# Ten instead of nine seven-product quads in each pair of column blocks, with a third sum buffer and one raw buffer fewer

## The chip, the core and the metric

The kernel runs on one core of a Trainium2 chip. The metric is the device time of one execution in microseconds (us), the median of several runs. The engines are PE (TensorE, matmuls), DVE (VectorE), ACT (ScalarE), POOL (GpSimd) and SP (SyncE, which here only issues DMAs).

## What is computed

One encoder layer for 256 positions of width 4096. The reference in its parts that matter here:

```python
h = layer_norm(x, emb_ln_g, emb_ln_b)                  # (256, 4096)
proj = h @ w_in[l]                                     # (4096, 22080 columns)
q_a, kv_a, dq, dk, dv, g_mla, g_dswa, r_mla, r_dswa = jnp.split(proj, IN_OFFSETS, axis=-1)
a = mla_attention(q_a, kv_a, ...)
y_mla = (a * silu(g_mla)) @ w_o_mla[l]
b = dilated_mixture(dq, dk, dv, rel_bias)
y_dswa = (b * silu(g_dswa)) @ w_o_dswa[l]
out = (sigmoid(r_mla) * y_mla + sigmoid(r_dswa) * y_dswa) @ w_out[l]
h = layer_norm(DEEPNORM_ALPHA * h + out, ln_g[l], ln_b[l])
```

The change is all in the big product `h @ w_in`, for 34 of its blocks of 512 columns.

## The kernel before

**Precision.** Every fp32 product is made of three matmuls on operands split into a high part and a rest: high times high, high times low, low times high. For a weight tile ACT writes the high part (`q_hi`), DVE then subtracts it from the raw tile and writes the rest (`q_low`, in the same bytes as `q_raw`).

**Pairs and quads.** 34 column blocks are taken as 17 pairs (p = 0 to 16). The 4096 rows of the weights are taken in 16 steps for each pair (q = 0 to 15), so that a step, a *quad*, is a 2x2 arrangement of products: two halves of the positions by two column blocks, over two row tiles of 128. The number of a quad over all pairs is g = 16p + q; its raw weights are one load of 1 MB into `q_raw[g % RAWS]`. A quad is done in one of two ways:

- *direct* (`direct_quad`): eight products, 24 matmuls of 128x512;
- *seven-product* (`seven_quad`, Strassen-Winograd): seven products, 21 matmuls. It wants three sums of the quad's weights (the first made in place by an accumulating DMA that POOL issues, `first_sum`; the others by two DVE subtractions, `quad_sums`, into `q_sum`), their high part on ACT and their rest on DVE (`q_sum_low`), and sums of the left operand (`t_hi`, `t_lo`), made once ahead of the pairs by `t_values`, one piece for each q in `SEVEN`.

`SEVEN` lists the q that are done with seven products: nine of the sixteen. Results gather in two sets of four PSUM banks. After a pair ACT copies the first of them out, and DVE combines the rest in `mixed_out` and `direct_out`, four adds each.

**What sets the order.** Each engine's program is written out in order; semaphores join them. SP issues the load of quad g when the raw buffer is free: `raw_free`, after the matmuls of quad g - RAWS that read `q_low` (for q = 0 after all of that quad). POOL issues the accumulating DMA of a seven-product quad when its load has landed. DVE takes for each g: the sums of quad g+1 if that is a seven-product quad (`sums_late` puts them behind instead for one q), then in q = 2 `direct_out` of the pair before, then `quad_low(g)`. `quad_low` waits for ACT's `quad_high(g)`, which waits until PE has done quad g-3 (three `q_hi` buffers). PE waits for `q_lo_ready` at the start of each quad.

**The first pair** starts while the section before it ("start") ends, so its raw buffers come free one by one: buffers that share bytes with that section's weight ring wait for `slot_done`, the one that holds the latent keys waits for `kva_stored`, the last, over `qa_sb`, for `qa_stored`. **After the last pair** the section "gates" begins; ACT may write the fourth slot of its ring only when the last pair's `c_fourth` is stored (`fourth_stored`), and POOL reads latent keys and queries back.

## Time and profile before

| | us |
|---|---|
| median of 3 runs | 2677.81 (2677.27 to 2680.55) |
| the profiled execution | 2677.33 |
| its span, first to last instruction | 2675.5 |
| PE busy | 2640.5 (99%) |
| DVE busy | 2061.1 (77%) |
| ACT busy | 1352.8 (51%) |
| granted TensorE clock, mean over the span | 0.996 |

The profiled execution takes 1.8 us more than its span. Matmuls are pipelined: one of 128x512 is shown with 389 ns, but the next starts 227 ns after it, so PE's pace is read from starts, or from a stretch divided by its matmuls. The pairs run from 175.71 us to 1559.08 us of the span.

### The profile page before, as it was taken

Reading aid. Unit: us, or ns where it says so; the run is one execution under the profiler, and the core shown is the slowest. Engines: PE = TensorE matmul, PEld = TensorE weight load, DVE = VectorE, ACT = ScalarE, POOL = GpSimd, SP = SyncE. Lnnn points to the kernel's source line nnn. Section 1 sums busy time; section 2 is a strip of 40 time slices with the busy share of each in tenths; the row PEclk is TensorE's granted clock in tenths of the full one; section 3 lists DMA queues with packets and bytes.
Section 4 is the critical chain, followed back from the end, with each engine's and each line's share of the span. In section 5 each row is a group of like instructions: output and inputs, shape, how many; then the busy total and the mean of one; then the engine's idle time right before and its main releaser. Section 6 shows DMA issues by size and latency. Waiting matters only on the chain.

```text
span 2675.5 us, 32812 instructions
## 1 busy us (share of the span) xinstructions
PE 2640.5 (99%) x12300; PEld 2205.5 (82%) x12300; DVE 2061.1 (77%) x1970; ACT 1352.8 (51%) x1295; POOL 264.4 (10%) x371
## 2 busy tenths in 40 slices
PE   7999999999999999999999999999999999999998
PEld 5878888888888888888888889988888888888886
DVE  7769888898888898888898876765565566656557
ACT  5445555555555555555555555544444444433333
POOL 0010111101111101111101101110100100110000
PEclk9999999999999999999999999999999999999998
DMA  6587887878888888888788864356776777777765
GB/s 206 168 288 222 256 261 246 248 237 256 256 252 252 240 244 258 253 253 253 235 243 263 249 213 126 128 173 207 236 244 181 232 224 232 249 235 220 229 216 177
DMA packets 240264, 612.89 MB, mean 229 GB/s; under 512 B 17513, under 2 KB 34261, under 8 KB 240004
## 3 DMA queue, kind: packets, MB, share of 16 engines
...
## 4 chain that ended last, share of the span: by engine, by line
PE 95%; DVE 2%; DMA 1%; issue 1%; ACT 0%; SPq 0%; DVEq 0%; ACTq 0%
PE acc L608 13%; PE acc L610 13%; PE acc L609 13%; PE bank L632 4%; PE bank L628 4%; PE bank L633 4%; PE acc L633 3%; PE acc L628 3%; PE acc L632 3%; PE acc L667 3%; PE acc L671 3%; PE bank L667 3%; PE acc L670 3%; PE bank L670 3%; PE bank L671 3%; PE acc L616 3%
## 5 line engine op out<-in xcount | busy, mean ns | idle before, releaser
L1020 ACT ACTIVATE q_hi<-q_raw 128x2048 fp32r<-128x2048 f32 x272 | 522.3, 1921 | 545.5 <-PE bank L617 155.7
L1223 DVE TENSOR_TENSOR w_lo<-w_raw,w_hi 128x1024 fp32r<-128x1024 f32 (+2 forms) x448 | 504.5, 1139 | 295.1 <-ACT w_hi L979 292.1
L1306 DVE TENSOR_TENSOR q_low<-q_raw,q_hi 128x2048 fp32r<-128x2048 f32 x272 | 621.2, 2284 | 5.2 <-ACT q_hi L1020 5.2
L979 ACT ACTIVATE w_hi<-w_raw 128x1024 fp32r<-128x1024 f32 (+2 forms) x448 | 430.9, 982 | 299.2 <-PE acc L610 253.4
L608 PE MATMUL acc<-w_hi,oper_hi 128*128 128x512 f32 (+1 forms) x1072 | 410.7, 383 | 3.2 <-DVE w_lo L1223 3.1
L610 PE MATMUL acc<-w_hi,oper_lo 128*128 128x512 f32 (+1 forms) x1072 | 405.6, 378 | 0.0
L609 PE MATMUL acc<-w_lo,oper_hi 128*128 128x512 f32 (+1 forms) x1072 | 405.2, 378 | 0.0
L1310 DVE TENSOR_TENSOR q_sum_low<-q_sum,q_hi 128x1536 fp32r<-128x1536 f32 x153 | 267.6, 1749 | 0.0
L1824 POOL DMA_DIRECT2D q_raw<-q_raw x153 | 131.1, 857 | 1207.2 <-DMA q_raw<-in_w_in 1207.2
L1023 ACT ACTIVATE q_hi<-q_sum 128x1536 fp32r<-128x1536 f32 x153 | 227.4, 1487 | 16.2 <-DVE q_sum L1298 0.5
L608 PEld LDWEIGHTS acc<-w_hi,oper_hi 128*128 128x128 f32 x1072 | 201.3, 188 | 41.6 <-DVE w_lo L1223 5.2
L610 PEld LDWEIGHTS acc<-w_hi,oper_lo 128*128 128x128 f32 x1072 | 201.2, 188 | 37.6
L609 PEld LDWEIGHTS acc<-w_lo,oper_hi 128*128 128x128 f32 x1072 | 201.4, 188 | 35.8
L1295 DVE TENSOR_TENSOR q_sum<-q_raw 128x512 f32<-128x512 f32 x153 | 105.6, 690 | 121.2 <-PE bank L617 58.6
L1298 DVE TENSOR_TENSOR q_sum<-q_raw,q_sum 128x1024 f32<-128x1024 f32 x153 | 187.5, 1225 | 5.2
L632 PE MATMUL bank<-q_hi,oper_hi 128*128 128x512 f32 x432 | 168.0, 389 | 0.0
L633 PE MATMUL bank<-q_hi,oper_lo 128*128 128x512 f32 x432 | 168.0, 389 | 0.0
L632 PE MATMUL acc<-q_hi,oper_hi 128*128 128x512 f32 x384 | 149.4, 389 | 0.0
L633 PE MATMUL acc<-q_hi,oper_lo 128*128 128x512 f32 x384 | 149.4, 389 | 0.0
L628 PE MATMUL bank<-q_low,oper_hi 128*128 128x512 f32 x432 | 106.7, 389 | 0.0
L608 PE MATMUL acc<-w_hi,am_hi 128*128 128x512 f32 x256 | 103.2, 403 | 0.0
L610 PE MATMUL acc<-w_hi,am_lo 128*128 128x512 f32 x256 | 100.0, 391 | 0.0
...
## 6 DMA issues: line engine op xcount, KB each, us to landing
q_raw<-in_w_in SPq DMA_DIRECT2D x256, 1024.0 KB, 6.1
w_raw<-in_w_in SPq DMA_DIRECT2D x128, 512.0 KB, 4.5
w_raw<-in_w_out SPq DMA_DIRECT2D x128, 512.0 KB, 3.9
q_raw<-q_raw POOLq DMA_DIRECT2D x153, 256.0 KB, 5.3
...
```

Of the source, the lines that this page charges most:

```text
L608: pe.matmul(y, hi[:, k, tok(t)], wh, start=first, stop=False)
L609: pe.matmul(y, hi[:, k, tok(t)], wl, start=False, stop=False)
L610: ins = pe.matmul(y, lo[:, k, tok(t)], wh, start=False, stop=last)
L628: ins = pe.matmul(banks[2 * i + t], oper_hi[:, 2 * q + a, tok(t)], raw_lo[:, 2 * a + i, :], start=False, stop=False)
L632: pe.matmul(y, oper_hi[:, k, tok(t)], hi[:, 2 * a + i, :], start=False, stop=False)
L633: ins = pe.matmul(y, oper_lo[:, k, tok(t)], hi[:, 2 * a + i, :], start=False, stop=q == QUADS - 1 and a == 1)
L979: act.activation(w_hi[:, n % RING, 0:w], w_raw[:, n % RING, 0:w], ACT.Copy).then_inc(w_hi_ready, 1)
L1020: act.activation(q_hi[h][:, 0:4, :], q_raw[r][:, :, :], ACT.Copy).then_inc(q_hi_ready, 1)
L1023: act.activation(q_hi[h][:, 4:7, :], q_sum[sevens_before(g) % 2][:, :, :], ACT.Copy).then_inc(q_hi_ready, 1)
L1223: dve.tensor_tensor(w_lo[:, n % RING, 0:w], w_raw[:, n % RING, 0:w], w_hi[:, n % RING, 0:w].bitcast(F32), ALU.subtract).then_inc(w_lo_read ...
L1306: dve.tensor_tensor(q_low[r], q_raw[r], q_hi[h][:, 0:4, :].bitcast(F32), ALU.subtract).then_inc(q_lo_ready, 1)
L1310: dve.tensor_tensor(q_sum_low[m], q_sum[m], q_hi[h][:, 4:7, :].bitcast(F32), ALU.subtract).then_inc(q_lo_ready, 1)
```

## The change

`SEVEN` gets ten entries, (2, 3, 4, 6, 7, 8, 10, 11, 12, 14) for (2, 4, 5, 7, 8, 10, 11, 13, 14). In the first pair three of them (2, 3, 4) stay direct, so it has seven such quads and not nine. Over all pairs there are 167 and not 153. The sums get a third buffer, which takes the bytes of one raw buffer; raw buffers go from six to five. What lay over the bytes of the raw buffer that is gone (the latent keys) is read back later, after quad 270. The store of a pair's results is issued in q = 7 and not 8 of the next pair, since it goes by `SEVEN[4]`.

```diff
-SEVEN = (2, 4, 5, 7, 8, 10, 11, 13, 14)
+SEVEN = (2, 3, 4, 6, 7, 8, 10, 11, 12, 14)
 NQ = PAIRS * QUADS
-RAWS, HIS = 6, 3
-KVA_RAW, QA_RAW = 2, RAWS - 1
+RAWS, HIS, SUMS = 5, 3, 3
+QA_RAW = RAWS - 1
+FIRST_DIRECT = (2, 3, 4)
+
+
+def sevens(p):
+
+    return tuple(q for q in SEVEN if p or q not in FIRST_DIRECT)
 
 
 def is_seven(g):
 
-    return g % QUADS in SEVEN
+    return g % QUADS in sevens(g // QUADS)
...
-T_STEPS = (("qa0", 5), ("qa0", 8), ("qa0", 11), ("qa0", 14), ("kva0", 3), ("kva0", 6), ("kva0", 9), ("kva0", 12), ("kva1", 12))
+T_STEPS = (("qa0", 5), ("qa0", 8), ("qa0", 11), ("qa0", 14), ("kva0", 3), ("kva0", 6), ("kva0", 9), ("kva0", 12), ("kva1", 10), ("kva1", 13))
...
-        q_raw = [sb(f"q_raw{n}", at_, [P, 4, CW]) for n, at_ in enumerate((R_B, R_B + 8 * K, R_C + 16 * K, RINGS + 32 * K, RINGS + 40 * K, R_C + 24 * K))]
+        q_raw = [sb(f"q_raw{n}", at_, [P, 4, CW]) for n, at_ in enumerate((R_B, R_B + 8 * K, RINGS + 32 * K, RINGS + 40 * K, R_C + 24 * K))]
...
-        q_sum = [sb(f"q_sum{n}", SMALL + 3328 + n * 6 * K, [P, 3, CW]) for n in range(2)]
+        q_sum = [sb(f"q_sum{n}", at_, [P, 3, CW]) for n, at_ in enumerate((SMALL + 3328, SMALL + 3328 + 6 * K, R_C + 16 * K))]
...
                     if g == 0:
                         sp.wait_ge(rows_stored, 16)
-                    elif g == KVA_RAW:
-                        sp.wait_ge(kva_stored, 32)
-                    elif g in (3, 4):
-                        sp.wait_ge(slot_done, SEC["start"].per_slot - (2 if g == 3 else 0))
+                    elif g in (2, 3):
+                        sp.wait_ge(slot_done, SEC["start"].per_slot - (2 if g == 2 else 0))
                     elif g == QA_RAW:
                         sp.wait_ge(qa_stored, 32)
...
-                if m >= 2:
-                    before = [n for n in range(g) if is_seven(n)][-2]
+                if m == SUMS - 1:
+                    dve.wait_ge(kva_stored, 32)
+                if m >= SUMS:
+                    before = [n for n in range(g) if is_seven(n)][-SUMS]
                     dve.wait_ge(quad_done, before + 1)
...
-                    sums_late = q == SEVEN[0] + 1 if p else q == 1
+                    sums_late = q == SEVEN[0] + 1 and p > 0
...
-                if g == SEVEN[0]:
+                if g == 0:
                     pool.wait_ge(acc_free, 4)
                     pool.dma_start(qa_d[:, :, CW:2 * CW], qa_sb[:, :, CW:2 * CW]).then_inc(qa_stored, 16)
                 if g >= QUADS and g % QUADS == SEVEN[4]:
                     store_pair(g // QUADS - 1)
-            for buffer in (KVA_RAW, QA_RAW):
-                last_user = NQ - 1 - (NQ - 1 - buffer) % RAWS
-                pool.wait_ge(raw_free, last_user - last_user // QUADS)
-                if buffer == QA_RAW:
-                    pool.dma_start(qa_sb[:, :, :], qa_d[:, :, :]).then_inc(qa_loaded, 16)
-                else:
-                    pool.dma_start(kva_hi[:, :, :].bitcast(F32), kva_d[:, 0, :, :]).then_inc(kva_loaded, 16)
-                    pool.dma_start(kva_lo[:, :, :].bitcast(F32), kva_d[:, 1, :, :]).then_inc(kva_loaded, 16)
+            last_user = NQ - 1 - (NQ - 1 - QA_RAW) % RAWS
+            pool.wait_ge(raw_free, last_user - last_user // QUADS)
+            pool.dma_start(qa_sb[:, :, :], qa_d[:, :, :]).then_inc(qa_loaded, 16)
+            pool.wait_ge(quad_done, NQ - 1)
+            pool.dma_start(kva_hi[:, :, :].bitcast(F32), kva_d[:, 0, :, :]).then_inc(kva_loaded, 16)
+            pool.dma_start(kva_lo[:, :, :].bitcast(F32), kva_d[:, 1, :, :]).then_inc(kva_loaded, 16)
             store_pair(PAIRS - 1)
```

How this moves instructions shows best at three places. The first is DVE's program in the first pair, from the second quad's `q_low1` on; the number behind a name is the buffer's. Before:

```order
L1306 TENSOR_TENSOR q_low1_72<-q_raw1_66,q_hi2_79 128x2048
L1347 COPY qa_sb_97<-acc1 128x2x512
L1295 TENSOR_TENSOR q_sum0_80<-q_raw2_67 128x512
L1298 TENSOR_TENSOR q_sum0_80<-q_raw2_67,q_sum0_80 128x1024
L1306 TENSOR_TENSOR q_low2_73<-q_raw2_67,q_hi1_78 128x2048
L1310 TENSOR_TENSOR q_sum_low0_82<-q_sum0_80,q_hi1_78 128x1536
L1295 TENSOR_TENSOR q_sum1_81<-q_raw4_69 128x512
L1298 TENSOR_TENSOR q_sum1_81<-q_raw4_69,q_sum1_81 128x1024
L1306 TENSOR_TENSOR q_low3_74<-q_raw3_68,q_hi2_79 128x2048
L1295 TENSOR_TENSOR q_sum0_80<-q_raw5_70 128x512
L1298 TENSOR_TENSOR q_sum0_80<-q_raw5_70,q_sum0_80 128x1024
L1306 TENSOR_TENSOR q_low4_75<-q_raw4_69,q_hi0_77 128x2048
```

and of the changed kernel:

```order
L1312 TENSOR_TENSOR q_low1_71<-q_raw1_66,q_hi2_77 128x2048
L1353 COPY qa_sb_97<-acc1 128x2x512
L1312 TENSOR_TENSOR q_low2_72<-q_raw2_67,q_hi1_76 128x2048
L1312 TENSOR_TENSOR q_low3_73<-q_raw3_68,q_hi2_77 128x2048
L1312 TENSOR_TENSOR q_low4_74<-q_raw4_69,q_hi0_75 128x2048
L1301 TENSOR_TENSOR q_sum0_78<-q_raw1_66 128x512
L1304 TENSOR_TENSOR q_sum0_78<-q_raw1_66,q_sum0_78 128x1024
L1312 TENSOR_TENSOR q_low0_70<-q_raw0_65,q_hi1_76 128x2048
L1301 TENSOR_TENSOR q_sum1_79<-q_raw2_67 128x512
L1304 TENSOR_TENSOR q_sum1_79<-q_raw2_67,q_sum1_79 128x1024
```

The sums of quads 2, 4 and 5 are gone; the first sums are those of quad 6 (`q_sum0<-q_raw1`), and they stand ahead of quad 5's `q_low0`.

The second is DVE's program around the end of a pair, here from pair 0 to pair 1. `c_first`, `c_third` and `c_fourth` are the targets of `mixed_out` (from `acc` here) and `direct_out` (from `bank`). Before:

```order
L1317 TENSOR_TENSOR c_first_84<-c_first_84,acc0 128x512
L1319 TENSOR_TENSOR c_third_85<-c_first_84,acc1 128x512
L1321 TENSOR_TENSOR c_first_84<-c_first_84,acc1 128x512
L1322 TENSOR_TENSOR c_fourth_86<-c_third_85,acc1 128x512
L1295 TENSOR_TENSOR q_sum1_81<-q_raw0_65 128x512
L1298 TENSOR_TENSOR q_sum1_81<-q_raw0_65,q_sum1_81 128x1024
L1306 TENSOR_TENSOR q_low5_76<-q_raw5_70,q_hi1_78 128x2048
L1330 TENSOR_TENSOR c_fourth_86<-bank3,c_fourth_86 128x512
L1331 TENSOR_TENSOR c_third_85<-bank2,c_third_85 128x512
L1332 TENSOR_TENSOR c_first_84<-bank0,c_first_84 128x512
L1333 TENSOR_TENSOR c_first_84<-bank1,c_first_84 128x512
L1306 TENSOR_TENSOR q_low0_71<-q_raw0_65,q_hi2_79 128x2048
```

and of the changed kernel:

```order
L1301 TENSOR_TENSOR q_sum1_79<-q_raw3_68 128x512
L1304 TENSOR_TENSOR q_sum1_79<-q_raw3_68,q_sum1_79 128x1024
L1312 TENSOR_TENSOR q_low2_72<-q_raw2_67,q_hi1_76 128x2048
L1301 TENSOR_TENSOR q_sum2_80<-q_raw4_69 128x512
L1304 TENSOR_TENSOR q_sum2_80<-q_raw4_69,q_sum2_80 128x1024
L1336 TENSOR_TENSOR c_fourth_86<-bank3,c_fourth_86 128x512
L1337 TENSOR_TENSOR c_third_85<-bank2,c_third_85 128x512
L1338 TENSOR_TENSOR c_first_84<-bank0,c_first_84 128x512
L1339 TENSOR_TENSOR c_first_84<-bank1,c_first_84 128x512
L1312 TENSOR_TENSOR q_low3_73<-q_raw3_68,q_hi2_77 128x2048
L1316 TENSOR_TENSOR q_sum_low1_82<-q_sum1_79,q_hi2_77 128x1536
```

Quad 3 of a pair is now a seven-product quad, and its sums (`q_sum2<-q_raw4`) stand between `q_low2` of quad 1 and `direct_out`.

The third is SP's queue of loads at the first pair. Before:

```order
L564 DMA q_raw0_65<-in_w_in 128x2x1024 [waits rows_stored]
L564 DMA q_raw1_66<-in_w_in 128x2x1024
L564 DMA q_raw2_67<-in_w_in 128x2x1024 [waits kva_stored]
L564 DMA q_raw3_68<-in_w_in 128x2x1024 [waits slot_done]
L564 DMA q_raw4_69<-in_w_in 128x2x1024 [waits slot_done]
L564 DMA q_raw5_70<-in_w_in 128x2x1024 [waits qa_stored]
L564 DMA q_raw0_65<-in_w_in 128x2x1024 [waits quad_done]
L564 DMA q_raw1_66<-in_w_in 128x2x1024 [waits raw_free]
```

and of the changed kernel:

```order
L568 DMA q_raw0_65<-in_w_in 128x2x1024 [waits rows_stored]
L568 DMA q_raw1_66<-in_w_in 128x2x1024
L568 DMA q_raw2_67<-in_w_in 128x2x1024 [waits slot_done]
L568 DMA q_raw3_68<-in_w_in 128x2x1024 [waits slot_done]
L568 DMA q_raw4_69<-in_w_in 128x2x1024 [waits qa_stored]
L568 DMA q_raw0_65<-in_w_in 128x2x1024 [waits quad_done]
L568 DMA q_raw1_66<-in_w_in 128x2x1024 [waits raw_free]
```

Buffer 2 no longer waits for `kva_stored`; the buffer over `qa_sb` is now the fifth, not the sixth, and the first buffer to be used again is that of quad 5, not quad 6.

## Rows read from the trace of the kernel before

**Rows 1.** The page: the chain that ended last, by engine.

```profile
PE 95%; DVE 2%; DMA 1%; issue 1%; ACT 0%; SPq 0%; DVEq 0%; ACTq 0%
```

**Rows 2.** Busy by stretch, first two pairs: PE, PEld, DVE, ACT, POOL; clock, DMA, GB/s.

```profile
175.71:264.20 88.49, 83.39 (x358) 68.53 (x357) 72.95 (x51) 44.26 (x26) 9.28 (x11) 0.96 0.81 245
264.20:345.12 80.92, 80.92 (x358) 67.03 (x357) 72.46 (x52) 44.41 (x26) 9.38 (x12) 1.00 0.82 250
```

**Rows 3.** Chain of work in the first pair, 189 to 203 us: start, us, what.

```profile
183.70 5.67 DMA q_raw<-in_w_in
...
189.66 8.15 DMA q_raw<-q_raw
...
197.84 0.70 DVE q_sum L1295
...
199.71 2.29 DVE q_low L1306
...
202.05 1.22 PE acc L667 x2
```

**Rows 4.** Timeline of PE in the first pair: its one long idle stretch.

```profile
202.05 0.79 PE L667 MATMUL acc<-q_low,oper_hi 128*128 128x512 f32 x1 [5.09 <-DVE q_low L1306]
```

**Rows 5.** Busy time by stretch, as rows 2: the stretch at half clock.

```profile
199.90:206.60 6.70, 4.55 (x11) 3.59 (x12) 6.70 (x4) 3.21 (x2) 0.01 (x1) 0.50 0.75 180
```

**Rows 6.** Timeline of DVE from quad 1 to quad 3 of pair 6.

```profile
664.19 0.69 DVE L1317 TENSOR_TENSOR c_first<-c_first,bank 128x512 f32<-128x512 f32 x1 [1.14 <-ACT c_first L1031]
...
666.84 0.68 DVE L1295 TENSOR_TENSOR q_sum<-q_raw 128x512 f32<-128x512 f32 x1
...
668.70 2.29 DVE L1306 TENSOR_TENSOR q_low<-q_raw,q_hi 128x2048 fp32r<-128x2048 f32 x1
670.90 0.69 DVE L1330 TENSOR_TENSOR c_fourth<-acc,c_fourth 128x512 f32<-128x512 f32 x1
...
673.30 2.28 DVE L1306 TENSOR_TENSOR q_low<-q_raw,q_hi 128x2048 fp32r<-128x2048 f32 x1
675.50 1.75 DVE L1310 TENSOR_TENSOR q_sum_low<-q_sum,q_hi 128x1536 fp32r<-128x1536 f32 x1
677.16 2.28 DVE L1306 TENSOR_TENSOR q_low<-q_raw,q_hi 128x2048 fp32r<-128x2048 f32 x1
```

**Rows 7.** Timeline of PE: first matmuls of quads 14 and 15 of pair 5.

```profile
658.60 0.39 PE L667 MATMUL bank<-q_low,oper_hi 128*128 128x512 f32 x1
...
663.36 0.39 PE L628 MATMUL acc<-q_low,oper_hi 128*128 128x512 f32 x1
```

**Rows 8.** Timeline of SP: the loads that these two quads set free, and one earlier.

```profile
654.94 0.37 SPq L564 DMA_DIRECT2D q_raw<-in_w_in  x1
...
659.70 0.37 SPq L564 DMA_DIRECT2D q_raw<-in_w_in  x1
...
665.37 0.37 SPq L564 DMA_DIRECT2D q_raw<-in_w_in  x1
```

**Rows 9.** Timeline of POOL: the accumulating DMA of pair 6's quad 2.

```profile
655.48 0.85 POOL L1824 DMA_DIRECT2D q_raw<-q_raw  x1 [19.50 <-DMA q_raw<-in_w_in]
```

**Rows 10.** DMA issues of 654 to 656.5 us: KB, us from issue to landing.

```profile
q_raw<-in_w_in SPq DMA_DIRECT2D x1, 1024.0 KB, 5.6
q_raw<-q_raw POOLq DMA_DIRECT2D x1, 256.0 KB, 6.3
```

**Rows 11.** Issue to landing, all loads (L564) and all accumulating DMAs (L1824).

```profile
DMA to landing us min/median/max: 3.7/5.9/11.1
...
DMA to landing us min/median/max: 3.2/5.3/9.9
```

**Rows 12.** DVE's waits: who waited for whom, us in total, times, longest.

```profile
DVE q_sum L1295 <- DMA q_raw<-q_raw: 8.6, 3, 6.8
```

**Rows 13.** Timelines at the first "gates" slots: POOL's store, the matmul that waits.

```profile
1561.04 0.55 POOL L1834 DMA_DIRECT2D pair_blocks<-c_fourth  x1 [15.11 <-ACT c_fourth L1038]
...
1567.45 0.50 PE L608 MATMUL acc<-w_hi,oper_hi 128*128 128x512 f32 x1 [0.21 <-DVE w_lo L1223]
```

More of the change, by code:

```diff
@@ L316, in program @@
         R_A = RINGS + 48 * K
-        R_B = R_A + 40 * K
+        R_B = R_A + 44 * K
         R_C = R_B + 16 * K
@@ L339, in program @@
         t_val = sb("t_val", R_A + (4 * len(SEVEN) + 2) * K, [P, 4, P])
-        q_raw = [sb(f"q_raw{n}", at_, [P, 4, CW]) for n, at_ in enumerate((R_B, R_B + 8 * K, R_C + 16 * K, RINGS + 32 * K, RINGS + 40 * K, R_C + 24 * K))]
-        q_low = [sb(f"q_low{n}", at_, [P, 4, CW], F32R) for n, at_ in enumerate((R_B, R_B + 8 * K, R_C + 16 * K, RINGS + 32 * K, RINGS + 40 * K, R_C + 24 * K))]
+        q_raw = [sb(f"q_raw{n}", at_, [P, 4, CW]) for n, at_ in enumerate((R_B, R_B + 8 * K, RINGS + 32 * K, RINGS + 40 * K, R_C + 24 * K))]
+        q_low = [sb(f"q_low{n}", at_, [P, 4, CW], F32R) for n, at_ in enumerate((R_B, R_B + 8 * K, RINGS + 32 * K, RINGS + 40 * K, R_C + 24 * K))]
         q_hi = [sb(f"q_hi{n}", at_, [P, 7, CW], F32R) for n, at_ in enumerate((R_C, RINGS, RINGS + 14 * K))]
-        q_sum = [sb(f"q_sum{n}", SMALL + 3328 + n * 6 * K, [P, 3, CW]) for n in range(2)]
-        q_sum_low = [sb(f"q_sum_low{n}", SMALL + 3328 + n * 6 * K, [P, 3, CW], F32R) for n in range(2)]
+        q_sum = [sb(f"q_sum{n}", at_, [P, 3, CW]) for n, at_ in enumerate((SMALL + 3328, SMALL + 3328 + 6 * K, R_C + 16 * K))]
+        q_sum_low = [sb(f"q_sum_low{n}", at_, [P, 3, CW], F32R) for n, at_ in enumerate((SMALL + 3328, SMALL + 3328 + 6 * K, R_C + 16 * K))]
         c_first = sb("c_first", R_A + 4 * len(SEVEN) * K, [P, 2, CW])
@@ L652, in seven_quad @@
                 raw_lo, hi = q_low[g % RAWS], q_hi[hi_buffer(g)]
-                sum_lo = q_sum_low[sevens_before(g) % 2]
-                first, last = n == 0, n == len(SEVEN) - 1
+                sum_lo = q_sum_low[sevens_before(g) % SUMS]
+                first, last = q == sevens(p)[0], n == len(SEVEN) - 1
                 p2, p3, p4, x = direct_banks(p)
@@ L682, in column_pairs @@
                     for q in range(QUADS):
-                        if q in SEVEN:
+                        if is_seven(p * QUADS + q):
                             seven_quad(p, q)
@@ L1022, in quad_high @@
                     act.wait_ge(sums_ready, sevens_before(g) + 1)
-                    act.activation(q_hi[h][:, 4:7, :], q_sum[sevens_before(g) % 2][:, :, :], ACT.Copy).then_inc(q_hi_ready, 1)
+                    act.activation(q_hi[h][:, 4:7, :], q_sum[sevens_before(g) % SUMS][:, :, :], ACT.Copy).then_inc(q_hi_ready, 1)
             def first_product_out(p):
@@ L1289, in quad_sums @@
                 r, m = g % RAWS, sevens_before(g)
-                raw, out_ = q_raw[r], q_sum[m % 2]
+                raw, out_ = q_raw[r], q_sum[m % SUMS]
                 dve.wait_ge(s1_made[r], first_sums(g))
-                if m >= 2:
-                    before = [n for n in range(g) if is_seven(n)][-2]
+                if m == SUMS - 1:
+                    dve.wait_ge(kva_stored, 32)
+                if m >= SUMS:
+                    before = [n for n in range(g) if is_seven(n)][-SUMS]
                     dve.wait_ge(quad_done, before + 1)
@@ L1307, in quad_low @@
                 if is_seven(g):
-                    m = sevens_before(g) % 2
+                    m = sevens_before(g) % SUMS
                     dve.wait_ge(q_hi_ready, splits_before(g) + 2)
```

## The prediction

> **What bounds the kernel now.** I read the page first: PE has 95% of the chain that ended last [rows 1]. So what counts is how many matmuls PE does, and whether anything makes it wait that did not before. Then the busy time by stretch, cut at the pairs [rows 2]: the second pair takes 80.92 us, all of it busy, and it has 9 x 21 + 7 x 24 = 357 matmuls, so one costs 226.7 ns (the view counts one more that laps over the edge). I take all later pairs to be like it. A seven-product quad is thus 4.76 us, a direct one 5.44 us. The first pair takes 88.49 us for the same work: 7.57 us are lost there. The chain in that pair [rows 3] shows where: the load of quad 5 issued at 183.70, its accumulating DMA from 189.66 for 8.15 us, the sums, then `q_low` of quad 4, and PE starts quad 4 at 202.05 after 5.09 us of idleness [rows 4]. Right behind, the granted clock is half, that is 1.2 GHz, for 6.7 us [rows 5]. Since 7.57 is more than the idle time, the clock has the rest.
>
> **The change, part by part.**
>
> *Matmuls.* In 16 pairs one more quad is seven-product: 16 x 3 x 0.2267 = **-10.88 us**. In the first pair two fewer are: 2 x 3 x 0.2267 = **+1.36 us**. A later pair then has 354 matmuls, 80.24 us; the first 363, 82.28 us.
>
> *DVE's load.* From DVE's timeline [rows 6], start to start: sums 1.86 us (666.84 to 668.70), `q_low` 2.20, `q_sum_low` 1.66 (675.50 to 677.16), `mixed_out` 2.65 (664.19 to 666.84), `direct_out` 2.40. A pair has 16 `q_low`, and 10 times the sums and their rest: 35.2 + 35.2 + 5.1 = 75.5 us against PE's 80.24. That fits, with 4.8 us to spare (before 72.0 of 80.92). In a run of three seven-product quads DVE needs 3 x 5.72 = 17.2 us to PE's 14.3, but with the direct quad behind it 19.4 to 19.7, so a run is made good. Going through a pair by these durations, with ACT's high part following PE's end of quad g-3, `q_low` ends 0.9 to 3 us ahead of PE's need (0.9 in quad 5, about 1.2 in quads 7 and 9) if the sums' data are there. The third buffer lets the third sum of a run start before the first is used up. I cost DVE's own work at nothing; its cover is these 0.9 us.
>
> *The raw buffers.* This is where it can go wrong. A load is issued 1.10 us after the start of the seven-product quad that frees its buffer (658.60, 659.70), 2.01 us after that of a direct one (663.36, 665.37) [rows 7, 8]. Now it is freed by quad g-5, not g-6, so each load starts some 5 us later against its use. Let T be the time from that issue to the landing of the accumulating DMA. Then sums take 1.9 us (from 189.66 + 8.15 = 197.81, to 199.71), and PE starts 2.34 us after `q_low` starts (202.05) [rows 3]: 4.2 us together, and they concern PE's quad g-1, since the sums of g stand ahead of `q_low(g-1)`. So for quads 6, 10 and 14 (buffer freed by a direct quad, four quads until the need, one of them direct): T may be 4.76 x 3 + 5.44 - 2.01 - 4.2 = 13.5 us. For quads 7, 8, 11 and 12: 14.4 us. For quad 3 `direct_out` comes in between too: 4.76 + 3 x 5.44 - 1.10 - 4.2 - 2.4 = 13.4 us. Quads 2 and 4 have more.
>
> What T is: a load takes 5.9 us in the median, an accumulating DMA 5.3, and 0.3 us lie between (183.70 + 5.67 to 189.66) [rows 3, 11]: 11.5 us. The slower ones show why: the accumulating DMA of quad 2 lands at 655.48 + 6.3, the load issued beside it at 654.94 + 5.6 [rows 8 to 10], so it comes 1.3 us behind the next load. T is then the distance of two loads (4.5 to 5.7 us), a load, and 1.3 us. With a load of 5.9 that is 11.7 to 12.9 us, under every limit; with one of 7 it is 12.8 to 14.0 and passes that of quad 3 (distance 5.7) by 0.6; with the longest accumulating DMA, 9.9, T is 16.1. Before, DVE waited for such a DMA three times in all, 6.8 of 8.6 us in the wait above [rows 12], so nothing of this showed. The DMA engines were busy for 0.82 of a pair [rows 2] and get a tenth accumulating DMA. Bounds for a later pair: 0 (T stays at 12.9), and 2.6 us (16.1 against 13.5; a stall gives the loads behind it time, so within a pair the largest excess counts, not the sum). The rows lie nearer to the lower end. I take 0.4 us a pair, a quarter of the pairs late by 1 to 2 us: 16 x 0.4 = **+6.4 us**.
>
> A page speaks on the same point. The Trainium skill (DMA: Bandwidth & Descriptors, section Anatomy of one DMA) gives a DMA about 2.0 us and its bytes at 436 GB/s. By that, called an estimate, a load is 4.4 us, the accumulating one 2.6, T 7.3, and no pair would ever wait: the sum would be 6.4 us lower. The trace does not agree: 5.9 and 5.3 in the median. The same page of the Trainium skill (section Latency and other measured facts) has HBM latency rise from 0.2 to 2 us under high load, which speaks against a change that adds traffic and removes a buffer; the longest load here, 11.1 us, fits that.
>
> *The first pair.* The 7.57 us go, since the sums of quads 2, 4 and 5 do: **-7.57 us**. What is late next is quad 6. Its sums stand ahead of quad 5's `q_low`. The load of quad 4 still waits for the stored queries, until 183.7, as quad 5's did [rows 3]; quads 5 and 6 follow within 1 us; that of quad 7 comes at 188.6 (quad 2 starts at 175.71 + 2 x 5.44, plus 2.01). Quad 6 is the third of three loads, so I put its landing near 194.4, its accumulating DMA 1.3 us behind the load of quad 7, at 199.5. PE would need quad 5 at 175.71 + 5 x 5.44 = 202.9, and gets it at 199.5 + 4.2 = 203.7. I take **+1.0 us**. Bounds: 0 (landing before 198.7), and with 8.15 us [rows 3] for the DMA from 194.7 it is 202.9 + 4.2 - 202.9 = 4.2, to which 2.5 (7.57 - 5.09) come if the clock falls again.
>
> *The tenth `t_values`* adds some 2.5 us of DVE work ahead of the pairs, which lies beside the last slots of "start"; `q_low` of quad 0 should end near 174.9, under 1 us ahead of PE. Cost 0; without that cover up to 1 us.
>
> *The end.* POOL reads the latent keys back at about 1553 us and not earlier, 1 MB on the queue in which `c_fourth` is stored at 1561.04; the fourth slot already waits for that store, 0.21 us [rows 13]. At 5.9 us, a 1 MB load's median [rows 11], the keys have landed by then. I take **+0.3 us** (0 to 2.6).
>
> Sum: -10.88 + 1.36 - 7.57 + 1.0 + 6.4 + 0.3 = **-9.4 us**. From the profiled execution's 2677.33 that is 2667.9. The median of the runs shown is 0.5 us higher, so I predict **2668.4 us** (-0.35%).
>
> **The rivals.**
>
> *All hidden.* The accumulating DMAs come in time in every pair, and at the first pair too. For it: a T of 11.5 by the medians. Against it: quad 3 needs its neighbour's load under 6.4 us. Sum: -10.88 + 1.36 - 7.57 + 0.3 = -16.8, 2661.0 us.
>
> *The first pair stalls as before.* Its accumulating DMA takes its 8.15 us and the clock falls: 4.2 + 2.5 instead of 1.0, 2674.1 us. For it: three loads bunch up behind the stored queries exactly as before. Against it: two accumulating DMAs fewer run beside them. The Trainium skill (TensorE: Matmul & The Clock Gate, section Terms) reckons a throttled stretch at its length times the share of pulses lost, here 6.7 x 0.5 = 3.4 us; rows 2 and 4 give 2.5, since PE was idle for part of it. By the page this case would end 0.9 us later.
>
> *The gain is eaten.* T exceeds its limit by about a microsecond in most pairs, 1.0 us each: 9.6 us more than in the forecast, 2678 us, no change. For it: quads 10 to 12 come in a run behind the 1 MB of stores that POOL issues in quad 7, with only quad 9 direct to let the queues empty.
>
> *Slower.* The same mechanism where every pair is late by 1.6 us at one quad: 16 x 1.6 = 25.6 for 6.4, 2687.6 us. It decides from 1.3 us a pair on (+5.4 us over before); T would have to be 14.8 us in each pair, where the medians add up to 11.5.
>
> *DVE becomes the bound.* By the sum above it cannot unless its operations grow by 6%; I give it no chance of its own.
>
> **How the numbers follow.** A measurement of this kernel tells some 0.2%, 5.4 us, from no change. Forecast (small waits, -5.4 to -14) 0.48; all hidden 0.20; first pair as before 0.06; gain eaten 0.18; slower 0.08. Faster is the first two and a third of the next: 0.70. Same 0.22. Slower 0.08. For 8 in 10 the range goes from the all-hidden case, 2660.5, to where half of "gain eaten" is in, 2677.0. The forecast's own range is 2663.5 to 2672.
>
> **What would show it.** In the changed profile: matmuls in the pairs fewer by 42; a later pair of 80.24 us where nothing waits, and PE idle ahead of a `q_low` matmul at quads 2, 5, 9 or 10 where it does, with DVE's sums waiting for `q_raw<-q_raw`; the first pair near 83.3 us with at most a short idle stretch at quad 5 and the clock at 1.00; the pairs' end some 10 us earlier. The prediction is wrong if later pairs stand above 81 us, if the clock falls again in the first pair, or if "gates" waits for its fourth slot by more than 1 us.

## The result and the profile after

The changed kernel takes 2691.60 us in the median of seven runs (2685.40 to 2700.58), the kernel before 2677.97 us in eight runs. An eighth run of the changed kernel, disturbed (6877.29 us), is left out; with it the median would be 2693.89. The ratio is 1.0053, with an interval of 1.0040 to 1.0066. It is slower by half a per cent, where I had predicted 2668.4 us. The profiled execution is one of the slower ones, 2696.74 us with a span of 2694.9.

The page of the changed kernel, the chain that ended last:

```profile
PE 73%; DMA 12%; DVE 11%; issue 3%; ACT 0%; SPq 0%; DVEq 0%; ACTq 0%
```

Against [rows 1] PE has lost 22 points of the chain, to DMA and DVE. Busy time by stretch, columns as [rows 2]: the first pair, the second, and the other fifteen.

```profile
175.65:259.13 83.48, 83.16 (x365) 67.84 (x363) 65.36 (x45) 40.99 (x24) 8.40 (x10) 1.00 0.83 252
259.13:341.20 82.07, 81.00 (x355) 66.21 (x354) 75.61 (x55) 45.38 (x27) 10.23 (x13) 1.00 0.85 250
341.20:1577.97 1236.77, 1216.59 (x5312) 994.32 (x5311) 1133.33 (x809) 695.21 (x427) 153.16 (x196) 1.00 0.83 247
```

The first pair takes 83.48 us, near the forecast's 83.3, with the clock at full speed. The later sixteen take 82.07 + 1236.77 = 1318.84 us where their matmuls need 16 x 80.24 = 1283.8. So 35.0 us are lost there, 2.2 us a pair, and I had put down 0.4. It is not a quarter of the pairs that are late: 15 of the 16 lose something, from 0.7 to 6.7 us. The waits of the changed kernel (who waited for whom, us in total, times, longest) say for what:

```profile
ACT q_hi L1027 <- DVE q_sum L1304: 94.7, 57, 7.1
ACT q_hi L1024 <- DMA q_raw<-q_raw: 86.4, 29, 5.8
DVE q_sum L1301 <- DMA q_raw<-q_raw: 55.7, 39, 5.5
...
PE acc L671 <- DVE q_low L1312: 6.6, 7, 1.8
PE bank L632 <- DVE q_low L1312: 6.1, 9, 2.3
PE acc L632 <- DVE q_low L1312: 4.8, 8, 0.9
PE bank L671 <- DVE q_low L1312: 3.8, 6, 1.8
```

DVE waits 39 times for an accumulating DMA, 55.7 us, where [rows 12] has 3 times and 8.6 us. The three before are all in the first pair; of the 39 now, 36 are in later pairs. Behind DVE, PE stands still for 21.3 us. Issue to landing, all loads and then all accumulating DMAs of the changed kernel, beside [rows 11]:

```profile
DMA to landing us min/median/max: 3.6/5.8/11.7
...
DMA to landing us min/median/max: 3.2/6.3/10.8
```

An accumulating DMA takes 1.0 us more in the median than before (6.3 for 5.3), a load 0.1 less. I paired each load with its accumulating DMA in both traces. T, from the load's issue to the accumulated landing, has in the later pairs a median of 11.8 us before (144 quads, 22 of them over 13.4 us, longest 16.5) and 12.0 us after (160 quads, 45 over 13.4, longest 17.3). So the whole time has hardly grown, and long ones were there before. This is the longest of the kernel before, quad 11 of pair 14: SP's timeline, POOL's timeline, the DMA issues at 1350.3, and DVE's timeline.

```profile
1343.10 0.37 SPq L564 DMA_DIRECT2D q_raw<-in_w_in  x1
...
1350.29 0.86 POOL L1824 DMA_DIRECT2D q_raw<-q_raw  x1 [1.86 <-DMA q_raw<-in_w_in]
...
q_raw<-q_raw POOLq DMA_DIRECT2D x1, 256.0 KB, 9.4
...
1361.99 0.69 DVE L1295 TENSOR_TENSOR q_sum<-q_raw 128x512 f32<-128x512 f32 x1 [0.61 <-PE bank L617]
```

The data landed at 1350.29 + 9.4 = 1359.7 us, 16.6 us after 1343.10, and DVE came for them 2.3 us later. The sixth raw buffer had covered 16.5 us without a trace in any table of waits.

What a late DMA does now is seen in the changed kernel's pair 13, which begins at 1252.77 us. DVE's timeline, and then the matmul at which PE waits, the first of quad 5:

```profile
1256.30 0.69 DVE L1301 TENSOR_TENSOR q_sum<-q_raw 128x512 f32<-128x512 f32 x1 [1.35 <-DMA q_raw<-q_raw]
...
1258.17 0.68 DVE L1336 TENSOR_TENSOR c_fourth<-bank,c_fourth 128x512 f32<-128x512 f32 x1
...
1260.57 2.28 DVE L1312 TENSOR_TENSOR q_low<-q_raw,q_hi 128x2048 fp32r<-128x2048 f32 x1
...
1264.43 2.28 DVE L1312 TENSOR_TENSOR q_low<-q_raw,q_hi 128x2048 fp32r<-128x2048 f32 x1
...
1270.35 2.29 DVE L1312 TENSOR_TENSOR q_low<-q_raw,q_hi 128x2048 fp32r<-128x2048 f32 x1
...
1276.09 2.28 DVE L1312 TENSOR_TENSOR q_low<-q_raw,q_hi 128x2048 fp32r<-128x2048 f32 x1
...
1278.43 1.89 PE L632 MATMUL acc<-q_low,oper_hi 128*128 128x512 f32 x7 [0.34 <-DVE q_low L1312]
```

The sums of quad 3 start when their data land. From there DVE has no idle time worth the name until `q_low` of quad 5 at 1276.09, 19.8 us later, and PE follows 2.34 us behind. PE could have begun quad 5 at 1252.77 + 2 x 5.44 + 3 x 4.76 = 1277.93. So the data of quad 3 had to land by 1277.93 - 2.34 - 19.8 = 1255.8. Its load was issued at about 1243.7 (1.10 us after the start of quad 14): T may be 12.1 us here and not 13.4. In this pair T was 12.6, and quad 5 begins 0.5 us late.

The same holds in all sixteen later pairs. What T of quad 3 has above 12.1 us is, to some 0.1 us, what PE loses at the starts of quads 2, 4 and 5 together:

| pair | T of quad 3 | above 12.1 | lost at quads 2, 4 and 5 |
|---|---|---|---|
| 15 | 10.5 | 0 | 0.0 |
| 8 | 12.0 | 0 | 0.0 |
| 13 | 12.6 | 0.5 | 0.5 |
| 10 | 13.0 | 0.9 | 0.9 |
| 6 | 14.4 | 2.3 | 2.2 |
| 5 | 15.2 | 3.1 | 3.0 |

Up to 13.3 us all of it is lost at quad 5; what is above that is lost at quad 2. This is 14.6 us of the 35.0. Another 7.4 us go in quads 6 and 7 (a loss in a quad is what its start and that of the next are too far apart), for the data of quad 8: its accumulating DMA is the next that POOL issues behind the stores of the pair before, its T has a median of 14.8 us against my limit of 14.4, and PE is late in the six pairs where it is over 15.5.

The clock fell once in the later pairs, behind the longest of these waits. PE's timeline, and a stretch behind it:

```profile
720.40 2.51 PE L632 MATMUL bank<-q_low,oper_hi 128*128 128x512 f32 x8 [2.33 <-DVE q_low L1312]
...
722.00:725.00 3.00, 3.00 (x9) 2.32 (x8) 3.00 (x2) 2.46 (x2) 0.00 (x0) 0.50 0.39 72
```

Granted 0.50, 1.2 GHz. The two quads there, the one before the wait's end and the one behind it, took 7.25 and 7.18 us for 4.76 and 5.44: 4.2 us over, of which 2.33 are idle time.

At the first slots of "gates", the answer to [rows 13], POOL's timeline, two of its DMA issues with KB and us to landing, and PE's timeline:

```profile
1572.83 0.54 POOL L1859 DMA_DIRECT2D kva_hi<-latent_keys  x1 [7.83 <-PE bank L621]
1573.36 0.53 POOL L1860 DMA_DIRECT2D kva_lo<-latent_keys  x1
1579.76 0.55 POOL L1840 DMA_DIRECT2D pair_blocks<-c_fourth  x1 [5.87 <-ACT c_fourth L1042]
...
kva_lo<-latent_keys POOLq DMA_DIRECT2D x1, 512.0 KB, 9.5
...
pair_blocks<-c_fourth POOLq DMA_DIRECT2D x1, 256.0 KB, 5.3
...
1587.44 0.50 PE L612 MATMUL acc<-w_hi,oper_hi 128*128 128x512 f32 x1 [1.31 <-DVE w_lo L1227]
```

The wait is 1.31 us, 1.1 more than before.

### The profile page after: what moved, and what is told of

Same layout as the page of the kernel before. It is cut to its first block, busy times and chain, and to the rows that moved or that the text cites. A ratio compares the mean times of both kernels' runs of the same rounds, so it can differ in the third digit from the quotient of the medians.

```text
span 2694.9 us, 32834 instructions
## 1 busy us (share of the span) xinstructions
PE 2643.2 (98%) x12258; PEld 2192.8 (81%) x12258; DVE 2107.4 (78%) x2018; ACT 1366.3 (51%) x1310; POOL 276.6 (10%) x385
## 3 DMA queue, kind: packets, MB, share of 16 engines
q0 software_dynamic: 41936, 105.84, 16.5%
## 4 chain that ended last, share of the span: by engine, by line
PE 73%; DMA 12%; DVE 11%; issue 3%; ACT 0%; SPq 0%; DVEq 0%; ACTq 0%
PE acc L612 13%; PE acc L614 13%; PE acc L613 13%; DMA q_raw<-q_raw 7%; DMA q_raw<-in_w_in 5%; DVE q_low L1312 4%; PE bank L632 2%; PE bank L637 2%; PE bank L636 2%; DVE q_sum_low L1316 2%; PE acc L671 2%; PE bank L671 2%; PE acc L632 2%; PE acc L636 2%; PE acc L637 2%
## 5 line engine op out<-in xcount | busy, mean ns | idle before, releaser
L1027 ACT ACTIVATE q_hi<-q_sum 128x1536 fp32r<-128x1536 f32 x167 | 247.8, 1484 | 95.3 <-DVE q_sum L1304 94.7
L1316 DVE TENSOR_TENSOR q_sum_low<-q_sum,q_hi 128x1536 fp32r<-128x1536 f32 x167 | 292.4, 1751 | 0.0
L1830 POOL DMA_DIRECT2D q_raw<-q_raw x167 | 143.1, 857 | 1201.8 <-DMA q_raw<-in_w_in 1201.8
L1304 DVE TENSOR_TENSOR q_sum<-q_raw,q_sum 128x1024 f32<-128x1024 f32 x167 | 204.6, 1225 | 5.8
L1301 DVE TENSOR_TENSOR q_sum<-q_raw 128x512 f32<-128x512 f32 x167 | 114.7, 687 | 56.5 <-DMA q_raw<-q_raw 55.7
L636 PE MATMUL bank<-q_hi,oper_hi 128*128 128x512 f32 x384 | 150.1, 391 | 0.0
L637 PE MATMUL bank<-q_hi,oper_lo 128*128 128x512 f32 x384 | 150.1, 391 | 0.0
L636 PE MATMUL acc<-q_hi,oper_hi 128*128 128x512 f32 x320 | 124.5, 389 | 0.0
L637 PE MATMUL acc<-q_hi,oper_lo 128*128 128x512 f32 x320 | 124.5, 389 | 0.0
L632 PE MATMUL bank<-q_low,oper_hi 128*128 128x512 f32 x384 | 97.0, 395 | 6.1 <-DVE q_low L1312 6.1
```

The source lines that it names most:

```text
L632: ins = pe.matmul(banks[2 * i + t], oper_hi[:, 2 * q + a, tok(t)], raw_lo[:, 2 * a + i, :], start=False, stop=False)
L636: pe.matmul(y, oper_hi[:, k, tok(t)], hi[:, 2 * a + i, :], start=False, stop=False)
L637: ins = pe.matmul(y, oper_lo[:, k, tok(t)], hi[:, 2 * a + i, :], start=False, stop=q == QUADS - 1 and a == 1)
L1027: act.activation(q_hi[h][:, 4:7, :], q_sum[sevens_before(g) % SUMS][:, :, :], ACT.Copy).then_inc(q_hi_ready, 1)
L1316: dve.tensor_tensor(q_sum_low[m], q_sum[m], q_hi[h][:, 4:7, :].bitcast(F32), ALU.subtract).then_inc(q_lo_ready, 1)
```

## The experiments

Twelve kernels, each timed beside the kernel before, which took 2676.4 to 2677.8 us in the medians. The changed kernel's 2691.60 us, with which they are compared below, was timed beside 2677.97. The expectations of the first four call the theory A: accumulated data come late, by more than DVE's slack can make good. I had not yet settled whether buffers, order or queue make them late.

**e1, DVE adds the direct products ahead of the sums.**

```
+ if p and q == 2: direct_out(p - 1)
  if g + 1 < NQ and is_seven(g + 1) and not sums_late: quad_sums(g + 1)
- if p and q == 2: direct_out(p - 1)
```

> One edit to the changed kernel: in q = 2 of a pair DVE does direct_out of the pair before ahead of the sums of quad 3, not behind them. Theory A (late data passed on): DVE has no idle time from the landing of quad 3's accumulating DMA to quad 5's q_low, so what it waits there reaches PE at quad 5; direct_out needs nothing of that DMA and fills the wait of about 1.4 us. The losses at quads 1, 4 and 5 of the later pairs (3.8 + 10.4 + 2.4 us in the profile of the changed kernel) go for the most part: 10 to 16 us faster than the changed kernel, about 2680 us. Rival B (DVE simply has too much work in a pair): the work is the same, no change, 2690 to 2697 us. Rival C (the stores in quad 7 are the cause): no change, quads 6 to 10 lose as before.

2681.64 us (2674.94 to 2689.18), ratio 1.001 (1.000 to 1.002): 10 us of the 14 come back. With DVE doing its 2.4 us of additions while it waits for quad 3's data, it is less behind at quad 5. The profile is of the slowest of its eleven runs (2689.18): even there the loss in quad 1 is gone (3.8 us in the changed kernel), and quads 4 and 5 together lose 10.1 us for 12.8. What is left stands in quads 4 to 7 and in 12 and 13.

**e2, the stores of a pair's results one seven-product quad later in POOL's queue.**

```
- if g >= QUADS and g % QUADS == SEVEN[4]:
+ if g >= QUADS and g % QUADS == SEVEN[5]:
```

> One edit to the changed kernel: POOL issues the store of the pair before behind the accumulating DMA of quad 8 instead of quad 7. Rival C (the stores stand ahead of quad 8's accumulating DMA in POOL's queue, 14.8 us from load issue to its landing in the median): that time falls by 2 to 3 us and the losses at quads 8 to 10 (7.6 us in all) go, 5 to 8 us faster, about 2687 us. Theory A gives the same sign with less, since quad 4 and 5 (12.8 us) stay: 0 to 5 us faster. Rival B: no change.

2709.39 us (2697.94 to 2711.61), ratio 1.0121 (1.0106 to 1.0137), 18 us slower than the changed kernel. The profile is of the fastest of its four runs (2697.94), so it shows little of that. In it the losses in quads 6 and 7 are gone (7.4 us over all pairs in the changed kernel, 0 here), with T of quad 8 down from 14.8 to 13.7 us in the median, but 3.2 us more are lost in quad 4, 3.6 more in quad 12, and 1 to 1.5 more in quads 1 and 9. Moving the stores moves the late quads. Why the sum grows I have not settled.

**e3, six raw buffers and two sum buffers, with the changed kernel's ten quads.** The sums of the third quad of a run then wait until the first is used up, and stand behind `q_low`.

```
- RAWS, HIS, SUMS = 5, 3, 3
+ RAWS, HIS, SUMS = 6, 3, 2
- sums_late = q == SEVEN[0] + 1 and p > 0
+ sums_late = q + 1 in (4, 8, 12)
```

> The changed kernel with six raw buffers and two sum buffers again; the sums of the third quad in a run (4, 8, 12) are made behind q_low of the second, since their buffer is free only then. Ten seven-product quads a pair stay. Theory A (five raw buffers make the data late): loads are issued a quad earlier, PE has nothing to wait for, later pairs take 80.24 us, 2661 to 2666 us, 10 us and more below the kernel before. Rival B (DVE has too much work): later pairs stay above 81.5 us, 2685 us and more, the more so with fewer sum buffers.

2712.14 us (2711.95 to 2712.26), ratio 1.0128 (1.0113 to 1.0144). My number fell, but for another reason than late data. The waits:

```profile
DVE q_sum L1302 <- PE bank L624: 33.7, 26, 1.7
DVE q_sum L1302 <- PE acc L624: 30.9, 24, 1.7
...
PE bank L635 <- DVE q_low L1313: 17.6, 26, 0.7
PE acc L635 <- DVE q_low L1313: 16.2, 24, 0.7
```

DVE waits 50 times for PE, and PE 50 times for DVE: three runs of three in each pair, the same 0.7 us each time, and every later pair takes 83.3 to 83.5 us. T was up to 19.6 us in this kernel, and no sum waited for it in any pair but the first. So a run of three, with its third sums behind `q_low`, does need the third sum buffer, which is what the change had bought with the raw one.

**e4, no accumulating DMAs.** It leaves out the first of the three weight sums of each seven-product quad; DVE, and ACT likewise, wait for the load alone.

```
- if is_seven(g):
-     first_sum(g)
...
- dve.wait_ge(s1_made[r], first_sums(g))
+ dve.wait_ge(q_loaded[r], quad_arrivals(g))
```

> The changed kernel without the accumulating DMAs: the first weight sum of each seven-product quad is left out (its output is not that of the reference), DVE and ACT wait for the load alone. DVE, ACT and PE do the same work. Theory A: the data come 5 to 7 us earlier, no waits in later pairs, 80.24 us each, about 2661 us. Rival B: DVE's work is what it was, pairs at 81.5 us and more, 2690 us. If it lies between, both have a part.

2660.68 us (2660.05 to 2661.05), ratio 0.9936 (0.9923 to 0.9950). The sixteen later pairs by stretch:

```profile
257.88:1541.88 1284.00, 1284.00 (x5666) 1063.22 (x5665) 1204.78 (x863) 733.95 (x454) 27.28 (x51) 1.00 0.64 222
```

1284.00 us, all of it busy. DVE is busy for 94% of it (1204.78) and holds nobody up. So the changed kernel's five raw buffers, its order and DVE's load are all right as long as the data are early. Its 35 us hang on the accumulating DMAs, by their own time or by the work that they put on the DMA engines, which are busy for 0.64 here and 0.83 there; this run does not part the two.

**e5, the kernel before with the first pair's part of the change alone.**

```
+ FIRST_DIRECT = (2, 4, 5)
- return g % QUADS in SEVEN
+ return g % QUADS in sevens(g // QUADS)
```

> The kernel before (nine seven-product quads, six raw buffers, two sum buffers) with the first pair's part of the change alone: quads 2, 4 and 5 of the first pair are direct. By my theory (the first pair was read rightly, and the whole loss lies in the later pairs) the first pair has 366 matmuls, 82.96 us, and a stall near the 1.2 us that the changed kernel showed there, in place of 88.49: 4.3 us faster than before, 2673.5 us, later pairs 80.92 us as before, the clock at full speed in the first pair. Rival (six buffers and the loads behind the stored queries keep a stall and the fall of the clock): the first pair stays above 86 us and the time within 2 us of before.

2674.42 us (2673.34 to 2677.18), ratio 0.9993 (0.9984 to 1.0001). In the profile the first pair takes 82.96 us with nothing lost and the clock at full speed, against 88.49 in [rows 2]. That is 5.5 us in the trace; in the medians it is 2.6, and the interval takes in no change. Of the difference, 1.7 us are lost behind the pairs, where the program is the same: that stretch takes 1118.2 us in this profile and 1116.6 before.

**e6, that kernel with five raw buffers and three sum buffers**, nine quads in the old order.

```
- RAWS, HIS = 6, 3
+ RAWS, HIS, SUMS = 5, 3, 3
```

> Nine seven-product quads in the order of before, but with five raw buffers and three buffers for weight sums, and the first pair as in the run of the first pair alone. Theory (DVE's lack of slack makes the lateness count, not the buffer by itself): with runs of two seven-product quads DVE may get the accumulated data some 14 us after the load's issue, so later pairs are at 80.92 us with at most 0.5 us of loss each: 2674 to 2682 us. Rival (five buffers are too few whatever the order, since five quads are 24.5 us and loads queue up): 2 us a pair are lost as in the changed kernel, 2705 us or more.

2693.47 us (2685.36 to 2700.06), ratio 1.0063 (1.0048 to 1.0078), as slow as the changed kernel. Against e5 a raw buffer has become a sum buffer, and 19 us are lost. With the buffer, the latent keys are read back later, as in the changed kernel; that costs 1.5 us of wait at "gates" here. The profile is of a faster run (2687.48, 14.0 us over e5's): 11.7 us of its loss lie in the pairs. Its waits for the accumulating DMAs, where e5 has 2.0 us in two:

```profile
DVE q_sum L1301 <- DMA q_raw<-q_raw: 127.5, 68, 6.0
```

The rival was right as to the cause. My theory, that DVE's lack of slack in runs of three was what mattered, fell here.

**e7, ten quads in runs of two, six raw and two sum buffers.** Quad 1 is added to the old nine, and DVE's `direct_out` moves from quad 2 to quad 1. The lines are shown against the kernel before; the latent keys are read back late, as in the changed kernel.

```
- SEVEN = (2, 4, 5, 7, 8, 10, 11, 13, 14)
+ SEVEN = (1, 2, 4, 5, 7, 8, 10, 11, 13, 14)
+ FIRST_DIRECT = (1, 2, 4, 5)
- if p and q == 2: direct_out(p - 1)
+ if p and q == 1: direct_out(p - 1)
```

> Ten seven-product quads in runs of two, 1-2, 4-5, 7-8, 10-11 and 13-14, so that six raw buffers and two sum buffers are enough; DVE adds the last pair's direct products in quad 1 and not in quad 2; the first pair has six seven-product quads. Theory (it is the run of three seven-product quads, which wants a third sum buffer in place of a raw one, that makes the data late and DVE unable to catch up): T may be over 14.5 us in each place, later pairs take 80.24 us with at most 0.3 us of loss, 2660 to 2666 us, and the spread over runs is that of before. Rival (DVE has no room for ten seven-product quads beside the two additions at the start of a pair, or the accumulating DMAs are simply too many): waits at quads 1 and 2, 0.5 us or more a pair, 2671 us or more.

2663.99 us (2663.18 to 2664.93), ratio 0.9952 (0.9939 to 0.9965). The sixteen later pairs:

```profile
259.05:1543.05 1284.00, 1284.00 (x5666) 1063.40 (x5665) 1209.28 (x862) 742.90 (x453) 162.35 (x208) 1.00 0.84 253
```

1284.00 us again, all busy, and now with all the accumulating DMAs: the DMA engines' busy share is 0.84, as high as in the changed kernel. Quad 8 of its pair 2 shows them no faster. SP's, POOL's and DVE's timelines and the DMA issues of e7:

```profile
350.59 0.37 SPq L571 DMA_DIRECT2D q_raw<-in_w_in  x1
...
358.14 0.88 POOL L1831 DMA_DIRECT2D q_raw<-q_raw  x1 [1.83 <-DMA q_raw<-in_w_in]
...
q_raw<-q_raw POOLq DMA_DIRECT2D x1, 256.0 KB, 9.8
...
369.48 0.69 DVE L1302 TENSOR_TENSOR q_sum<-q_raw 128x512 f32<-128x512 f32 x1 [0.61 <-PE bank L624]
```

T is 17.4 us (landed at 367.9), more than the changed kernel's longest, and DVE came 1.5 us after it. No sum in the later pairs waited for its data. Over all 160 quads T has a median of 12.3 us, against 12.0 in the changed kernel.

**e8, five raw buffers, runs of three, but quad 3 direct**, with `direct_out` ahead of the sums as in e1.

```
- SEVEN = (2, 3, 4, 6, 7, 8, 10, 11, 12, 14)
+ SEVEN = (2, 4, 5, 6, 8, 9, 10, 12, 13, 14)
```

> Ten seven-product quads with five raw and three sum buffers as in the changed kernel, but runs of three at 4-6, 8-10 and 12-14 and quad 2 alone, so that quad 3 is direct behind the addition of the direct products, which is put ahead of the sums. Theory (slack of DVE at quads 2 to 5 is what counts): T may be 13 us against 12.1 in the changed kernel, so most of the waits go, 0.2 to 0.8 us a pair are left, 2664 to 2674 us. Rival (the waits at quads 7 to 13 come from the queue of accumulating DMAs behind the stores, which stay): 1.2 us a pair or more, above 2680 us as with the addition put first alone.

2711.34 us (2705.66 to 2714.26), ratio 1.0128 (1.0114 to 1.0143). The theory's number fell, and the rival's place was right. Quads 4 and 5 lose 6.8 us over all pairs, but quads 7 and 8 lose 31. There the accumulating DMA of quad 9 stands behind the stores in the middle of a run: its T is 15.3 us in the median. I had reckoned with one T for all quads.

**e9, the first weight sum by POOL's arithmetic**, in the changed kernel.

```
- pool.dma_start(raw[:, 1, :], raw[:, 3, :], accum_op=ALU.add)
+ pool.tensor_tensor(raw[:, 1, :], raw[:, 1, :], raw[:, 3, :], ALU.add)
```

> The changed kernel with the first weight sum of each seven-product quad made by POOL's arithmetic (one 128x512 addition) in place of the accumulating DMA. POOL's additions of 128x256 take 0.83 to 0.91 us, so I estimate 1.8 us for one of 128x512 against 6.3 us for the DMA in the median. Theory (the accumulated data are late, and with five raw buffers nothing covers that): T falls to some 8 to 10 us, under every limit, later pairs take 80.24 us as without the DMAs, 2660 to 2665 us. Rival (POOL and DVE get in each other's way in the memory that both work on, so DVE, with 75.5 of 80.24 us used, becomes the bound): DVE's operations last longer, later pairs 82 us or more, 2690 us or more.

2780.27 us (2777.75 to 2780.98), ratio 1.0384 (1.0369 to 1.0398). The rival was right. DVE's timeline and POOL's, where they meet:

```profile
804.10 2.29 DVE L1312 TENSOR_TENSOR q_low<-q_raw,q_hi 128x2048 fp32r<-128x2048 f32 x1
806.31 2.85 DVE L1316 TENSOR_TENSOR q_sum_low<-q_sum,q_hi 128x1536 fp32r<-128x1536 f32 x1
809.08 1.92 DVE L1301 TENSOR_TENSOR q_sum<-q_raw 128x512 f32<-128x512 f32 x1
...
804.31 3.23 POOL L1830 TENSOR_TENSOR q_raw<-q_raw 128x512 f32<-128x512 f32 x1 [2.12 <-DMA q_raw<-in_w_in]
...
809.13 1.30 POOL L1830 TENSOR_TENSOR q_raw<-q_raw 128x512 f32<-128x512 f32 x1
```

The addition itself takes 1.29 us at its shortest here, and no sum in the later pairs waited for it, but DVE's operations that meet one grow by 1.1 to 1.2 us (2.85 for 1.75, 1.92 for 0.69), and POOL's wait in turn (3.23). A later pair takes 87.4 to 88.4 us. The Trainium skill (SBUF — State Buffer, section Who interferes with whom) says that a DVE instruction with two inputs in SBUF and a GpSimd instruction that reads SBUF contend for the one port pair that the two engines share, and that this pair is an exclusive lock; the trace agrees, with 1.1 us more for a DVE operation that meets a POOL operation of 1.3.

**e10, e7 with five raw and three sum buffers.**

```
- RAWS, HIS, SUMS = 6, 3, 2
+ RAWS, HIS, SUMS = 5, 3, 3
```

> The faster kernel (ten seven-product quads in runs of two, e7) with five raw and three sum buffers. With the run of the first pair alone, nine quads and five buffers, and e7 it makes a square of two orders by two numbers of buffers. Theory, as it now stands after nine quads with five buffers lost 19 us (the raw buffer alone carries the loss): the same loss or more, 15 to 45 us over e7, 2680 to 2710 us, with DVE's sums waiting for accumulating DMAs at most quads. Rival (the loss needs an order with little slack of DVE, runs of two are safe): within 3 us of e7's 2664 us.

2704.59 us (2703.29 to 2714.90), ratio 1.0102 (1.0087 to 1.0117). That closes the square:

| | six raw, two sum | five raw, three sum |
|---|---|---|
| nine quads | 2674.42 (e5) | 2693.47 (e6) |
| ten in runs of two | 2663.99 (e7) | 2704.59 (e10) |

The raw buffer is worth 19 us with nine quads (1.5 of them the read-back) and 41 us with ten. In the profile of e10, its slowest run (2714.90), 23.6 us are lost in quad 0 alone. DVE waits there for the data of quad 1 in 14 of the 16 pairs, with a T of 11.5 us in the median and 11.8 at most: the limit itself lies below the usual T. The tenth quad gains 10.4 us with six raw buffers and costs 11.1 with five.

**e11, e7 with seven seven-product quads in the first pair**, quad 5 among them.

```
- FIRST_DIRECT = (1, 2, 4, 5)
+ FIRST_DIRECT = (1, 2, 4)
```

> e7 with seven seven-product quads in the first pair (quads 5, 7, 8, 10, 11, 13, 14) in place of six: three matmuls fewer, 0.68 us. Theory: quad 5's sums come too late there as they did in the changed kernel's first pair, where 1.2 us were lost, so nothing is won: 2663.5 to 2665 us. Rival: the loads are in time with six buffers, 2663.3 us. The two differ by less than the whole time can tell; the first pair's own time in the profile decides, 84.1 against 82.28 us.

2661.78 us (2660.74 to 2662.48), ratio 0.9943 (0.9930 to 0.9957). The first pair takes 83.82 us with one idle stretch of 1.21 us, so as the theory said nothing is won in it. The median is yet 2.2 us under e7's; that gain is not in the pairs. The stretch behind them takes 1116.9 us in this profile and 1118.9 in e7's, of which the waits at "gates" explain 0.5 us (1.11 for 1.66). That stretch varied by 1.7 us between e5 and the kernel before too, so the 2.2 us stay unexplained.

**e12, e11 with the latent keys read back as early as before.**

```
+ for buffer in (KVA_RAW, QA_RAW):
+     last_user = NQ - 1 - (NQ - 1 - buffer) % RAWS
- pool.wait_ge(quad_done, NQ - 1)
  pool.dma_start(kva_hi[...], kva_d[:, 0, :, :])
```

> e11 with the latent keys read back where the kernel before reads them, behind the last use of their raw buffer, and not behind quad 270 in the queue right ahead of the last stores. The first matmul that waits in gates stands idle for 1.11 us in e11, 1.31 in the changed kernel, 0.21 before. Theory (the 1 MB of reads in that queue holds up the store of the fourth block): the wait goes back to 0.2 us, 0.9 us faster than e11, 2660.9 us. Rival (the wait comes from the pairs' end itself, whatever stands in the queue): 1.1 us of wait stay and the time is e11's 2661.8 us. The wait in the profile decides, since the times differ by less than runs do.

2661.00 us (2660.52 to 2661.46), ratio 0.9938 (0.9925 to 0.9952). POOL's timeline and PE's:

```profile
1514.93 0.56 POOL L1862 DMA_DIRECT2D kva_hi<-latent_keys  x1 [2.65 <-PE bank L674]
...
1545.35 0.55 POOL L1841 DMA_DIRECT2D pair_blocks<-c_fourth  x1 [15.01 <-ACT c_fourth L1045]
...
1551.90 0.50 PE L615 MATMUL acc<-w_hi,oper_hi 128*128 128x512 f32 x1 [0.18 <-DVE w_lo L1230]
```

The wait at "gates" is back at 0.18 us. It is the fastest kernel of the study, 15.5 us under the kernel before and 31 under the changed one. Its lead over e11, 0.8 us in the medians, fits the 0.9 us less of wait, but it is within the spread of e11's runs, so the wait and not the time shows the effect.

## Why the prediction was wrong

*Matmuls, -10.88 and +1.36.* Right. Where nothing waits (e4, e7) sixteen pairs take 1284.0 us for 1283.8.

*First pair, -7.57 and +1.0.* Right for the 7.57: 83.48 us for 83.3, and the clock stayed. The 1.0 was right by luck. It was to be lost at quad 5, but the data of quad 6 had landed by 198.7 us, not 199.5, and PE lost 0.2 us in quads 4 and 5; of the 1.2 us in all, 0.4 went in quads 6 and 7 and 0.6 in quads 12 and 13, where I had put nothing. With six such quads in place of seven (e5, e7) nothing is lost.

*The end, +0.3.* Mis-sized: 1.1 us (1.31 for 0.21). "The keys have landed by then" was false. The second of the two reads was issued at 1573.36 and took 9.5 us, to 1582.9, so `c_fourth`'s store, issued at 1579.76, ran beside it and took 5.3 us for 4.0 before. In e12 the reads are early and the store takes 4.2.

*DVE's load, 0.* Right by itself. It is 75.6 us a pair for 75.5, and e4 runs at PE's pace.

*The raw buffers, +6.4.* This is the step that failed: 35.0 us in the profiled run for 6.4. The mechanism was the one described, late accumulated data behind a shorter ring; its size was not, and two things in the reckoning were wrong.

First, "11.5 us: the medians" was taken for what T is, and "a quarter of the pairs late by 1 to 2 us" for its spread. One pair has ten such quads, so the longest of ten counts and not the median. In the kernel before, 22 of 144 quads already had a T over 13.4 us, 1.4 a pair, up to 16.5. Pairing loads and accumulating DMAs by quad in that trace, rather than looking at DVE's waits [rows 12], would have shown them. The few waits there said that six buffers cover a T of 16.5, not that T is short.

Second, the limits were worked out one by one, as if DVE were free when the data landed, and "its cover is these 0.9 us" was reckoned apart. It is the same slack. Quad 3's data have to be there by T = 12.1 for quad 5 to start in time, not 13.4 for quad 2, since DVE's queue from there has no gap for 19.8 us. A lateness is handed on until the next direct quads. Against 12.1 us the trace comes out to 0.1 us in every later pair, 14.6 us in all. For quad 2 itself the limit was nearly right: losses there begin at a T of 13.3. e1 shows this part: the same buffers, the same DMAs, two steps of DVE exchanged, 10 us.

Of the rivals, "slower" had the mechanism and nearly the size (2687.6), with 0.08. It was to decide from 1.3 us a pair on; the loss in the profile is 2.2. That it "would have to be 14.8 us in each pair, where the medians add up to 11.5" is the sentence that talked it down: 23 of 160 quads had over 14.4.

The cause is shown: without the accumulating DMAs the loss is gone (e4), with the sixth raw buffer it is gone with DMAs just as long (e7) and back without that buffer (e10), and taking the buffer away brings it about in the old order too (e6). Open is how the stores' place (e2, e8) shifts the long ones among the quads, and what makes single DMAs long.
